# Input tiles loaded over two queues ahead of the constants, and norm factors spread by transposes

## The reference, cut to what matters

```python
def rms_norm(x, g):
    xf = x.astype(jnp.float32)
    y = xf * lax.rsqrt(jnp.mean(xf * xf, axis=-1, keepdims=True) + EPS)
    return (y * g.astype(jnp.float32)).astype(x.dtype)
...
        x = x + swiglu_ffn(rms_norm(x, norm_ffn_g[layer]), w_ffn_in[layer], w_ffn_out[layer])
    return rms_norm(x, norm_final_g)
...
    return rms_norm_2(x, final_norm)
```

## Time and profile before

| what | value |
|---|---|
| median of 3 runs | 2547.4 us (2541.57 to 2550.29) |
| the profiled execution's own time | 2545.35 us |
| its span in the profile | 2543.5 us |
| PE busy | 2464.6 us, 97% of the span |
| DVE, ACT, POOL busy | 50%, 39%, 16% |
| PE's first matmul | at 16.57 us |
| PE's last gemm matmul starts | at 2524.70 us |

### The profile page before, as it was taken

One profiled execution on the slowest core, in us unless ns is written; L12 is line 12 of the kernel. 1 busy time (PEld: TensorE's weight loads), 2 busy tenths in 40 slices (PEclk: granted clock), 3 DMA queues, 4 the chain that ended last, 5 costly groups with the idle time before them and its releaser, 6 DMA issues.

```text
span 2543.5 us, 29069 instructions
## 1 busy us (share of the span) xinstructions
PE 2464.6 (97%) x11378; PEld 1983.4 (78%) x11378; DVE 1263.1 (50%) x1898; ACT 1004.6 (39%) x1634; POOL 395.3 (16%) x284
## 2 busy tenths in 40 slices
PE   7999999998989999999999999999999999999997
PEld 5766667777778887888888788888887777888886
DVE  5577744457786454533333533423577544444422
ACT  6666654335455243432223323322633333333221
POOL 0000000054410010111102111101455300111101
PEclk9999999999999999999999999999999999999998
DMA  5321234323446331333332233322321222333321
GB/s 164 96 59 54 71 99 163 99 91 117 143 134 211 121 128 47 98 93 100 99 103 97 75 100 100 99 91 91 98 67 58 84 100 67 100 100 99 98 94 49
DMA packets 171337, 251.56 MB, mean 99 GB/s; under 512 B 11200, under 2 KB 88256, under 8 KB 171200
## 3 DMA queue, kind: packets, MB, share of 16 engines
q1 hardware_dynamic: 171200, 249.70, 31.0%
HBM read 231.83 MB, written 16.78 MB: 98 GB/s over the span
## 4 chain that ended last, share of the span: by engine, by line
PE 82%; DVE 8%; issue 5%; ACT 4%; DMA 1%; POOL 1%; SPq 0%; DVEq 0%; ACTq 0%; POOLq 0%
PE bank L1060 80%; DVE W L1797 1%; DVE T L1805 1%; DVE wlo L1797 1%; DMA scr_z<-T 1%; ACT whi L1363 1%; PE bank L1140 1%; DVE SC L2412 0%; ACT pr L1455 0%; ACT qs L1363 0%; DMA zb<-scr_z 0%; DVE pr L1912 0%; DVE T L1797 0%; DMA cst<-in_cst 0%; ACT xp L1664 0%
## 5 line engine op out<-in xcount | busy, mean ns | idle before, releaser
L1060 PE MATMUL bank<-xh,whi 128*128 128x512 f32 x1784 | 720.2, 404 | 18.8 <-DVE wlo L1797 18.3
L1060 PE MATMUL bank<-xh,wlo 128*128 128x512 f32 x1784 | 699.1, 392 | 0.0
L1060 PE MATMUL bank<-xl,whi 128*128 128x512 f32 x1784 | 698.4, 391 | 0.0
L1797 DVE TENSOR_TENSOR wlo<-raw,whi 128x1024 fp32r<-128x1024 f32 (+2 forms) x382 | 473.0, 1243 | 327.4 <-ACT whi L1363 327.2
L1363 ACT ACTIVATE whi<-raw 128x1024 fp32r<-128x1024 f32 (+2 forms) x406 | 419.5, 1038 | 539.9 <-PE bank L1060 531.1
L1060 PEld LDWEIGHTS bank<-xh,whi 128*128 128x128 f32 x1784 | 337.3, 189 | 116.0 <-issue 30.1
L1060 PEld LDWEIGHTS bank<-xh,wlo 128*128 128x128 f32 x1784 | 336.6, 189 | 71.8
L1060 PEld LDWEIGHTS bank<-xl,whi 128*128 128x128 f32 x1784 | 337.6, 189 | 68.6 <-issue 3.8
L1797 DVE TENSOR_TENSOR T<-bank,R 128x512 f32<-128x512 f32 x90 | 61.7, 687 | 340.2 <-PE bank L1060 340.2
L1060 PE MATMUL bank<-hh,wlo 128*128 128x512 f32 x528 | 205.6, 389 | 0.0
L1060 PE MATMUL bank<-hl,whi 128*128 128x512 f32 x528 | 205.6, 389 | 0.0
(11 more groups left out here) (342 smaller groups left out, 3628.2 us busy)
## 6 DMA issues: line engine op xcount, KB each, us to landing
raw<-in_w_in SPq DMA_DIRECT2D x92, 512.0 KB, 3.7
raw<-in_w_ffn_in SPq DMA_DIRECT2D x88, 256.0 KB, 3.1
raw<-in_ffn_gate SPq DMA_DIRECT2D x88, 256.0 KB, 2.8
raw<-in_ffn_up SPq DMA_DIRECT2D x88, 256.0 KB, 3.0
raw<-in_ffn_down SPq DMA_DIRECT2D x44, 512.0 KB, 3.5
raw<-in_w_ffn_out SPq DMA_DIRECT2D x22, 512.0 KB, 3.5
raw<-in_w_xattn_kv SPq DMA_DIRECT2D x16, 512.0 KB, 4.0
raw<-in_w_kv_mem SPq DMA_DIRECT2D x16, 512.0 KB, 3.7
```

Of the source, the lines that this page charges most:

```text
L1060: return e.matmul(out, l, r, start=start, stop=stop, skip_group_check=skip)
L1797: return e.tensor_tensor(out, a, b, op)
```

## The change

Three edits. **The start:** tiles 0, 2 and 4 of `xT` are issued by ACT, at the head of its own queue, the others by SP, and the weight slots move up by one place each on SP. `identity` is gone (`identr` was used nowhere else). The two small steps that prepared `nsink` (ACT) and `gboth` (DVE) at the very start become one step `sinks`, placed ahead of the attention. **The norms:** `diagonals` is gone from DVE; `spread` and `h_spread` wait for `rn` alone and run one PE transpose for each column of `rn`, with that column repeated 128 times as its input. **The last norm:** `acc` holds squares 0 to 6, square 7 is summed over partitions by itself in a second group of four matmuls, and DVE adds the two columns; the factors are spread twice, first into a bank that DVE's `out` reads, then into one that ACT copies to `R` for POOL; POOL keeps tiles 0 and 3, DVE takes six; `fin_gain` of those two tiles moves up behind their squares.

```diff
@@ the list
         for k in range(8):
             step("x_in", k)
-            if k % 2:
-                load_to(1 + k // 2)
+            if k in (1, 3, 5):
+                load_to(2 + k // 2)
         step("constants")
...
+        step("sinks")
         step("mark", "qkv")
...
-        for k in (0, 3, 6):
-            step("fin_gain", k)
         side.new("rms", "fin")
-        tmp.new("diag", "fin")
-        step("rms", "fin")
+        side.new("last", "fin")
+        step("rms_last")
+        side.new("spread", "last")
+        step("spread_last")
         side.new("spread", "fin")
         step("mark", "Rfin")
         step("spread", "fin")
@@ PE
+            def rms_last():
+                rms("fin")
+                n, t = tmp("sq", "fin", 7)
+                u, b = side("last", "fin")
+                w.wait_ge(*free(side, "side", u))
+                w.wait_ge(*at("square", "fin", 7))
+                column_sums(b, t, S).then_inc(*up("rms_sum", ("last sum",)))
...
+            def across_partitions(b, rn, width):
+                for c in range(width // P):
+                    ins = e.transpose(b[:, chunk(c)], rn[:, c:c + 1].to_broadcast([P, P]), ident)
+                return ins
...
             def spread(tag):
                 u, b = side("spread", tag)
-                d, t = tmp("diag", tag)
-                width = SUMS[tag][1]
                 w.wait_ge(*free(side, "side", u))
-                w.wait_ge(*at("diag", tag))
-                mm(b[:, 0:width], ones, t[:, 0:width], True, True).then_inc(
-                    *up("spread", ("spread", tag), ("tmp", "free", d)))
+                w.wait_ge(*at("rn", tag))
+                across_partitions(b, Rn3 if tag == "fb2" else RNS[tag][0], SUMS[tag][1]).then_inc(
+                    *up("spread", ("spread", tag)))
@@ ACT
+            def x_in(k):
+                if k in (0, 2, 4):
+                    e.dma_start(xT[:, k, :], io["xT"][chunk(k), :]).then_inc(*T.up("act", f"d_x_early{k}", [("x in", k)], 16))
...
-            def identity():
-                w.wait_ge(*at("cst"))
-                copy(identr[:], ident).then_inc(*up("scan_act", ("identr",)))
@@ DVE
-            def diagonals(tag, rn):
...
-                for c in range(SUMS[tag][1] // P):
-                    ins = ts(t[:, chunk(c)], ident, rn[:, c:c + 1], None, ALU.mult)
...
+            def rms_last():
+                u, b = side("rms", "fin")
+                w.wait_ge(*at("rms sum", "fin"))
+                ts(Rn2, b[:, 0:4], 1.0 / 1024, EPS, ALU.mult, ALU.add).then_inc(*up("norm", ("rn2", 3)))
+                u, b = side("last", "fin")
+                w.wait_ge(*at("rn2", 3))
+                w.wait_ge(*at("last sum"))
+                stt(Rn1, b[:, 0:4], 1.0 / 1024, Rn2, ALU.mult, ALU.add).then_inc(*up("norm", ("rms mean", "fin")))
+                w.wait_ge(*at("rms sqrt", "fin"))
+                e.reciprocal(Rn1, Rn1).then_inc(*up("norm", ("rn", "fin")))
...
             def out(k):
                 if k in ON_POOL:
                     return
-                w.wait_ge(*at("R", "fin"))
+                u, b = side("spread", "last")
+                w.wait_ge(*at("spread", "last"))
                 w.wait_ge(*at("res", "fin", k))
-                stt(xT[:, k, :], xT[:, k, :], V("fin_2", k), R[:], ALU.mult, ALU.mult).then_inc(*up("out", ("out", k)))
+                stt(xT[:, k, :], xT[:, k, :], V("fin_2", k), b[:], ALU.mult, ALU.mult).then_inc(*up("out", ("out", k)))
```

More of the change, by code:

```diff
@@ L444, in evict @@
                 square(tag, k)
+                if tag == "fin" and k in ON_POOL:
+                    step("fin_gain", k)
                 if tag == "fb":
@@ L1112, in spread, with spread_last @@
                 u, b = side("spread", tag)
[L1113 to L1114 removed]
                 w.wait_ge(*free(side, "side", u))
[L1116 to L1118 removed]
+                w.wait_ge(*at("rn", tag))
+                across_partitions(b, Rn3 if tag == "fb2" else RNS[tag][0], SUMS[tag][1]).then_inc(
+                    *up("spread", ("spread", tag)))
+            def spread_last():
+                u, b = side("spread", "last")
+                w.wait_ge(*free(side, "side", u))
+                w.wait_ge(*at("rn", "fin"))
+                across_partitions(b, Rn1, S).then_inc(*up("spread", ("spread", "last")))
             def scores(i, pair):
@@ L1341, in h_spread @@
                 w.wait_ge(*free(side, "side", u))
-                w.wait_ge(*at("h diag", h))
-                mm(b[:], ones, osq[:], True, True).then_inc(*up("h_tail", ("h spread", h)))
-            does = {"mm": weight_tile, "rms": rms, "two_rms": two_rms, "spread": spread, "scores": scores, "p_turn": p_turn,
+                w.wait_ge(*at("rn", "h", h))
+                across_partitions(b, RNS["h"][0], S).then_inc(*up("h_tail", ("h spread", h)))
+            does = {"mm": weight_tile, "rms": rms, "rms_last": rms_last, "spread_last": spread_last, "two_rms": two_rms, "spread": spread, "scores": scores, "p_turn": p_turn,
                     "pv": pv, "turn": turn, "dt_turn": dt_turn, "cum": cum, "cb": cb, "state": state_, "difference": difference, "seg": seg, "within": within_,
@@ L1364, in copy, with sinks @@
                 return e.activation(out, in_, ACT.Copy, scale=scale)
-            def first():
-                w.wait_ge(*at("vec"))
+            def x_in(k):
+                if k in (0, 2, 4):
+                    e.dma_start(xT[:, k, :], io["xT"][chunk(k), :]).then_inc(*T.up("act", f"d_x_early{k}", [("x in", k)], 16))
+            def sinks():
                 copy(nsink[:], V("sink", 0, 16), -1.0).then_inc(*up("nsink", ("nsink",)))
@@ L1772, in fin_gain @@
                 copy(xT[:, k, :], xT[:, k, :], V("fin_2", k)).then_inc(*up("fin_gain", ("fin gain", k)))
-            does = {"vec": first, "constants": identity, "w_hi": weight, "x_split": x_split, "square": square, "rms": rms,
+            does = {"x_in": x_in, "sinks": sinks, "w_hi": weight, "x_split": x_split, "square": square, "rms": rms, "rms_last": lambda: rms("fin"),
                     "two_rms": two_rms, "spread": spread, "q_out": q_out, "k_out": k_out, "v_out": v_out,
@@ L2468, in out @@
                     return
-                w.wait_ge(*at("R", "fin"))
+                u, b = side("spread", "last")
+                w.wait_ge(*at("spread", "last"))
                 w.wait_ge(*at("res", "fin", k))
-                stt(xT[:, k, :], xT[:, k, :], V("fin_2", k), R[:], ALU.mult, ALU.mult).then_inc(*up("out", ("out", k)))
-            does = {"vec": first, "w_lo": weight, "x_lo": x_lo, "square": square, "rms": rms, "two_rms": two_rms,
+                stt(xT[:, k, :], xT[:, k, :], V("fin_2", k), b[:], ALU.mult, ALU.mult).then_inc(*up("out", ("out", k)))
+            does = {"sinks": sinks, "w_lo": weight, "x_lo": x_lo, "square": square, "rms": mean, "rms_last": rms_last, "two_rms": two_rms,
                     "turn_tables": turn_tables, "rotated": rotated, "score_max": score_max,
```

30 lines of the change are left out of this document (8 added, 22 removed).

## The result

| | before | after |
|---|---|---|
| median of 6 runs each | 2547.57 us (2541.57 to 2550.29) | 2532.94 us (2525.62 to 2536.75) |
| the profiled execution, and its span | 2545.35, 2543.5 us | 2534.28, 2532.5 us |
| PE's first matmul | 16.57 us | 8.85 us |
| last gemm matmul to the span's end | 18.80 us | 15.80 us |

The time after is 0.9942 of that before, interval 0.9926 to 0.9958: 14.6 us faster by the medians, 11.0 by the two profiled spans. Of those 11.0, 7.72 lie ahead of the first matmul (16.57 - 8.85) and 3.00 behind the last matmul of the last gemm (2543.5 - 2524.70 = 18.80 against 2532.5 - 2516.70 = 15.80). Only 0.3 is left for the 2508 us in between, where the norms were to bring most of 5.5. What became of it is the main question of the experiments.

The account below looks back on a forecast made before the run. PE, busy for 97% of the span, was taken to bound the kernel, with waits at the start and the end. Terms 7.2 + 5.5 + 2.2 = 14.9 us brought the median from 2547.4 to 2532.5 us, range 2525 to 2541.

Parts of the forecast that it names:

- start: Ahead of PE's first matmul: without the wait for the constants PE starts near 9.4 us; 7.2 us gained (6.2 to 8.2).
- norms: Spreads of the norms: four transposes at 0.44 us save 0.42 us for each full spread; 5.5 us in all.
- end: Behind POOL's last add: earlier spread and outputs, then eight tiles bound by transfers; 2.2 us gained (1.2 to 3.2).
- early bound: At the start: tile 1, third in SP's queue as tile 0 was, lands at 6.25 and PE starts at 8.4 us.
- late bound: At the start: tile 1 lands at 8.2, or the table load waits behind tile 0; PE at 10.35, 6.2 us gained.
- Rival A: At the start: transfers bind, tile 1 or the first slot lands at 12.9, PE starts at 15.1; 2538.2 us, chance 0.08.
- in between PE is full: Between start and end: PE busy 50.00 of 50 us, 222 matmuls at 0.225 us each.
- Rival B: In the norms: a transpose costs 0.2 us, so the spreads give only 1.0 us; 2537.0 us, chance 0.13.
- rival C: Behind spreads: PE's clock falls to 1.2 GHz, 2.65 us for each of 14 spreads; slower, 2569.6 us, chance 0.04.

Follow-up runs that it names:

- experiment 4: Kernel before with only the start's edits, but SP issuing all eight tiles of xT and no second queue: 2540.6 us, ratio 0.9969.
- Experiment 5: Changed kernel with every spread but the last done twice into the same bank, as extra work for PE: 2534.49 us, ratio 0.995.
- 2: Kernel before with only the spreads changed, diagonals out and transposes in, the last norm spread once: 2540.46 us, ratio 0.9977.
- 8: Changed kernel with a small ACT copy of nsink that loads ACT's table ahead of the wait for tile 0: 2532.3 us in one run.
- 3: Kernel before with only the end's edits; start as before, middle norms keep their diagonals: 2542.34 us, ratio 0.9984.
- experiment 6: Changed kernel with the last tiles multiplied and sent in the order in which they are ready (1, 2, 4, 0, 5, 6, 3, 7): 2526.61 us, ratio 0.9926.
- experiment 7: Kernel before and changed kernel, both unedited, profiled once more: 2542.11 and 2529.9 us. Its weaker rival: the change may make falls of PE's clock likelier.

## Why the prediction was right

The forecast, 2532.5 us, is 0.4 from the median, which is luck: the measured difference is known to 4 us to either side, and the terms are less exact than 0.4. The norms brought less than costed, start and end more.

| term | predicted (bounds), us | measured, us |
|---|---|---|
| start | 7.2 (6.2 to 8.2) | 7.7 |
| norms | 5.5 (1.0 to 8.6) | about 4.9 |
| end | 2.2 (1.2 to 3.2) | 3.0 |
| sum | 14.9 | about 15.6; 14.6 (10.7 to 18.9) by the medians |

**The start** was right in its mechanism: PE waited for the constants, with nothing else needed that late. The first matmul at 8.85 lies between the bounds of 8.4 and 10.35, whose last link, 2.15 us from the second `xh` to PE, measured 2.17. The early bound's reason also held: tile 1, third in SP's queue, sets the start, and landed at 6.66 where the row of before had 6.25. The late bound was the truth of another kernel, the one without the second queue (10.26). The second queue did more than the prediction allowed it. Windows of the start, in the changed kernel and in experiment 4:

```profile
4.00:8.80 4.80, 0.00 (x0) 0.00 (x0) 2.11 (x4) 4.13 (x6) 0.00 (x0) 1.00 1.07 397
...
4.00:8.80 4.80, 0.00 (x0) 0.00 (x0) 0.61 (x1) 2.64 (x4) 0.00 (x0) 1.00 0.97 326
```

The DMA engines moved 397 GB/s with two issuing queues and 326 with one. Over all profiles that stretch has 394 to 399 in the seven with two queues and 309 to 333 in the five with one; from 9 to 12 us both kinds reach 396 to 400 (before, changed, 4). The Trainium skill ("DMA: Bandwidth & Descriptors", Rules for kernel authors) says that spreading transfers over issuing engines doesn't help bandwidth. This start differs from that, and the measurement decides. By that rule the gain should have been 6.2, the late bound; it is 6.31 with one queue and 7.72 with two. The 1.41 between them came by way of tile 0, which lands at 4.5 and not at 6.1 and so takes the table load off the path; tile 1 lands at about 6.7 in both. How much of tile 0's lead is its place in the order and how much the rate, no run took apart. Rival A, a first matmul at 15.1, is refuted. PE then ran on as costed; only the count of its first, slower matmuls (8 at 0.43 us apart in the changed profile, 14 in its repeat) varied, worth up to about a microsecond of luck.

**The norms** are the term whose places were mis-sized. The price was right: 0.445 us for four transposes (predicted 0.44), and 0.42 to 0.44 saved at each of the eight full spreads in gemms, 3.4 in all, as costed. The heads of the second mixer were not worth it: from one spread to the next the lead grows by 0.11, 0.13 and 0.11, and only behind the last by 0.43, which is 0.8 in place of 1.7. The step that failed there is that an instruction taken from PE's queue is worth its own time: it isn't where PE then waits. Experiment 5 shows where the rest went, into PE's wait for `SC` (1.2 us between two heads before, 1.5 after, 1.2 with the doubled spreads). The prediction had read that "in between PE is full" from one window of 50 us, and the text ahead of it that PE waits in two stretches only; the earlier trace rows has 9.5 us of waits in the heads alone. The second memory norm gave 0.22, as costed. At the first the clock's steps cover it in most profiles. In five whose clock falls there as in the kernel before, the lead grows by 0.5 to 0.6 from 634 to 690 with transposes (2, 5, 8) and shrinks by 0.1 to 0.2 with the old spreads (3, 4). About 0.5 is my estimate for it, and 4.9 for the term.

Rival B, 0.2 us for a transpose, is refuted by 0.11 in three kernels, rival C by the clock of 1.00 behind eight. The price of C took fourteen matmuls of the start to be at 1.2 GHz; the earlier trace rows gives 1.00 as the granted clock there, so that level was read from their spacing (5.8 us for fourteen) and not from a row of the clock.

**The end** came out 0.8 us better than costed, inside its bounds. The links, counted from POOL's last add (2526.67 before, 2518.67 after): the sums end at 2.0 and not 2.7, because PE's clock was at 2.4 GHz and not near 1.2 as in the old sums; DVE's first output starts at 3.9 and not 4.5; the first tile is sent at 6.8 and not 7.35; the end follows 7.0 after that and not 7.4. DVE's tile takes 0.744 us where the row of an instruction that reads a bank had 0.692:

```profile
L1825 DVE SCALAR_TENSOR_TENSOR xT<-xT,vec,bank x6: 743/744/748, 2522.6 to 2525.9; 128x512 f32<-128x512 f32 x6
```

That the end is set by transfers from SP's first issue on was stated and is shown by experiment 6. That this issue waited for a tile of POOL, with a tile of DVE ready 2.2 us before, was in the prediction's numbers (2531.2 + 0.7 against 2534.05) without being drawn out.

**The profiled difference,** 11.0 us, was not wrong either: start and end give 10.7, the norms about 4.9, and the steps of the clock took back some 4.6 in that pair of executions. The repeats differ by 15.4 - 3.2 = 12.2. Six runs each put it at 14.6; the interval, 10.7 to 18.9 us, holds all of these. It also leaves room for the weaker rival of experiment 7, by which falls of the clock would cost a few us on average.

## What to carry to other kernels

Where an engine's first useful instruction waits, look at what stands ahead of it in its queue: a copy that nobody needed yet waited here for constants issued behind all the tiles and cost 6.3 us, and a table load behind a wait for data cost 1.28 in one version. An instruction taken from the busiest engine is worth its time only where that engine does not wait next. At the end, send results in the order in which they are made, since here the end came 7.0 us after the first issue, whichever tile went first. And before the difference of two profiles is explained by the code, profile each kernel once more: at three places of this one the same code was seen at two granted clocks, and that moved its instructions by about 2 us.

## What the hardware did that I had not expected

- A transpose of one column repeated 128 times costs what one of a full tile costs, 0.11 us among gemm matmuls.
- Small matmuls can keep or lose the clock behind an equal gap: eight transposes after 0.77 us of idle PE took 1.97 us at a granted clock of 0.50, in another kernel after 0.78 us 1.12.
- With one issuing queue the DMA engines moved 309 to 333 GB/s from 4.0 to 8.8 us (five profiles), with two 394 to 399 (seven profiles).
- The same transfer, third in SP's queue, landed 4.9 to 5.1 us after its issue in five profiles, and 5.8 in a sixth, whose ACT loads its table earlier. Second in ACT's queue it took 4.8.
